# Expert weights fetched in whole rows, eight feature sums open at once, gathers and scatters moved

## The chip, the cores and the metric

One core of one Trainium2 chip runs the whole program in a single launch. The metric is the device time of one execution in microseconds (us). A difference of 0.3% is 12 us here.

## The reference, cut to what matters

The model has two layers over 512 latent tokens and, in the first layer only, 256 context tokens, all of width 1024, in float32. The change touches the last step of each layer, the expert-choice feed-forward:

```python
cap = EC_CAPACITY * N // N_EXPERTS                      # 64 tokens of 512, 32 of 256
aff = softmax(h @ w_router)
gate, idx = lax.top_k(swapaxes(aff, 1, 2), cap)         # each of 16 experts picks its tokens
xe = h[bidx, idx]
hid = silu(xe @ w_gate[e]) * (xe @ w_up[e])             # 1024 -> 1024 features
ye = (hid @ w_down[e]) * gate
return zeros_like(h).at[bidx, idx].add(ye)
```

Each expert's three matrices are 1024 x 1024. In layer 0 an expert handles 64 latent and 32 context tokens (M = 96, `with_ctx`), in layer 1 the 64 latent ones (M = 64).

## The kernel before, in words

The program is a list of phases with a barrier between them; `experts0` and `experts1` are the two that the change touches, both made by `expert_loop(l, with_ctx)`. Each works through 8 pairs of experts: pair 0 is written out, pairs 1 to 6 are a hardware loop on every engine (`Fori`), pair 7 is written out, so that the first pair has no scatters to do and the last no gathers.

**Weights.** SyncE streams them through a ring of 6 slots of 1 MB. A chunk is 256 of a matrix's 1024 columns over all 8 blocks of 128 rows, so each partition gets 8 runs of 1 KB. A pair takes 24 chunks: per expert `e` four times gate and up in turn, then four of down. A slot is loaded again (L1881, L1882) when the matmuls of the chunk in it are done.

**Gate and up (L1960).** Weights are the stationary operand, the gathered tokens `XE` the moving one. One chunk gives two blocks of 128 features; each block is a sum over the 8 row blocks, finished before the next is begun, in a bank of its own that alternates (banks 2, 3 for gate, 4, 5 for up). ScalarE takes silu of gate (L2001) and VectorE multiplies by up into `HT` (L2039) chunk by chunk. In the trace each float32 matmul is two weight loads and two matmul records.

**Down (L1976).** `HT` is stationary, 256 columns of the weights move; ScalarE and VectorE copy each chunk's result out of banks 6 and 7 (L2007 latent rows into `YEL`, L2049 context rows into `YEC`).

**Gather (L1924, L1928; VectorE L2020, L2023).** The tokens of the next pair are picked by a matmul of `X` with a selection matrix, one block of 128 features at a time, 4 matmuls and in layer 0 another 2 of the context; VectorE scales and shifts the result into `XE`. Two gathers, into banks 0 and 1, follow each down chunk of the pair's second expert.

**Scatter (L1944; VectorE L2031).** One matmul per 128 tokens and 512 columns puts the previous pair's result back in token order, 12 steps in layer 0 and 8 in layer 1, and VectorE adds it to `YACC`. They follow the gate and up chunks of the pair's first expert, one or two (layer 0) or one (layer 1) at a time, and alternate banks 6 and 7. GpSimd copies their stationary operand `PTCUR` (L2069, L2071).

**Order.** Every hand-over is a counting semaphore in `ex`; `at(x, i, n)` is its value at step n of pair i, and `credit` is how many steps a producer may run ahead, which is the number of buffers: 2 for gathers (`xe`), scatters (`added`) and the rest. L2154 is the barrier between phases.

Of the kernel before, what the change touches and what calls it, by code (L numbers as in the profile page):

```python
# [24 lines left out]
P = 128  # L25
D = 1024
# [86 lines left out]
def program(nc, t, upto=None, dumps=()):  # L113

    es = ExitStack()
    with es:
# [1710 lines left out]
        PAIR_CHUNKS = 2 * 3 * D // CW  # L1827
# [3 lines left out]
        def expert_loop(l, with_ctx):  # L1831
# [6 lines left out]
            SIL = [A(18944 + 2 * M * i, 2, M) for i in range(2)]  # L1838
            HT = [A(19328 + KB * M * i, KB, M) for i in range(2)]
# [34 lines left out]
            def load(sp, i, j, free=None):  # L1874
# [3 lines left out]
                src = flat[bass.ds(l * NE + 2 * i + e, 1), :, :, c * CW:(c + 1) * CW].rearrange("a p k n -> (a p) k n")  # L1878
# [3 lines left out]
                sp.dma_start(slot(s), src).then_inc(w_full[s], 16)  # L1882
# [27 lines left out]
            def wslot(j):  # L1910
                return slot(first + j)

            def scatter_steps(q):
                return range(q * NS // 8, (q + 1) * NS // 8)

            def pe():
                def gather(i, k):

                    nc.tensor.wait_ge(ex["xe"], at("xe", i, k + 1))
                    bk = bank[k % 2]
                    for n in range(LT):
                        mm = nc.tensor.matmul(bk[:, 0:2 * CAP_L], X[:, CT + n, k * P:(k + 1) * P],  # L1924
                                              PL[:, n, bass.ds(i * (2 * CAP_L), 2 * CAP_L)], start=n == 0, stop=n == LT - 1)
                    if with_ctx:
                        for n in range(CT):
                            mm = nc.tensor.matmul(bk[:, 2 * CAP_L:2 * M], X[:, n, k * P:(k + 1) * P],  # L1928
                                                  PC[:, n, bass.ds(i * (2 * CAP_C), 2 * CAP_C)], start=n == 0, stop=n == CT - 1)
                    mm.then_inc(ex["gather"], 1)  # L1930

                def scatter(i, n):
                    tl, hf = outs[n]
                    if n == 0:
                        nc.tensor.wait_ge(ex["dl"], at("dl", i, 8 + 2))
                        if with_ctx:
                            nc.tensor.wait_ge(ex["dc"], at("dc", i, 8 + 2))
                        nc.tensor.wait_ge(ex["ptcur"], at("ptcur", i, per["ptcur"]))
                    nc.tensor.wait_ge(ex["added"], at("added", i, n + 1))
                    if tl < CT:  # L1940
                        w, y = PTCUR[0:2 * CAP_C, S_LAT + tl * P:S_LAT + (tl + 1) * P], YEC[0:2 * CAP_C, :]
                    else:
                        w, y = PTCUR[:, (tl - CT) * P:(tl - CT + 1) * P], YEL
                    nc.tensor.matmul(bank[6 + n % 2][:, :], w, y[:, hf * 512:(hf + 1) * 512], start=True,  # L1944
                                     stop=True).then_inc(ex["scatter"], 1)

                def pair(i, first_pair, last_pair):
                    nc.tensor.wait_ge(ex["xe"], at("xe", i, KB + 2))
                    for e in range(2):
                        xe = XE[:, :, e * M:(e + 1) * M]  # L1950
                        for c in range(4):
                            n = 4 * e + c
                            for w, x, free in (("gate", 2, "silu"), ("up", 4, "hid")):
# [9 lines left out]
                                if e == 0 and not first_pair:  # L1963
                                    for m in scatter_steps(2 * c + (w == "up")):
                                        scatter(i - 1, m)
# [285 lines left out]
```

## Time and profile before

| | us |
|---|---|
| median of 3 runs | 4068.06 |
| lowest, highest | 4056.97, 4069.73 |
| span of the profiled execution, first to last instruction | 4066.2 |
| experts of layer 0, first to last gate matmul of pairs 1 to 6 | 1455.33 to 2148.45 |
| layer 1, start of pair 1 in the trace | 3298.71 |

TensorE is busy 86% of the span, VectorE 28%, ScalarE 14%, GpSimd 11%, and 126 GB/s are read on average. In the rows below PE is TensorE's matmul side and PEld its weight loads, DVE is VectorE, ACT ScalarE, POOL GpSimd, SP SyncE. A row of the page or of a group view ends in: busy us, mean ns of one | idle time of the engine before them and what ended it; "issue" is idle time that no recorded wait explains. PEclk is the granted TensorE clock, where 1.00 is 2.4 GHz and 0.50 is 1.2 GHz. No time of a profiled execution other than its span is at hand.

### The profile page before, as it was taken

To read this page: it belongs to the slowest core of one execution; us is meant where nothing else is said; L and a number is where in the kernel's file an instruction comes from. 1 tells how busy PE (TensorE), PEld (TensorE's weight loads), DVE (VectorE), ACT (ScalarE), POOL (GpSimd) and SP (SyncE) were. 2 spreads that over 40 slices of the span, in tenths; PEclk is the share of its full clock that TensorE was granted. 3 is DMA by queue.
4 is the path that set the end of the run, shared out by engine and by line. 5 is a ranking of instruction groups with operands and counts; after the bars stand their busy time and mean duration, and the time that the engine had idled before them with its cause. 6 is when DMAs were issued, how large, how long until landed. Compare 5 with 4: busy or idle time off the path is not lost. (4 is left out here: it accounts for less than half of the span.)

```text
span 4066.2 us, 49080 instructions
## 1 busy us (share of the span) xinstructions
PE 3505.4 (86%) x20674; PEld 2738.5 (67%) x20674; DVE 1128.0 (28%) x2115; ACT 568.3 (14%) x1182; POOL 449.8 (11%) x366
## 2 busy tenths in 40 slices
PE   7989977888798999999999498994665899999995
PEld 2445564877675787888888266573564688888884
DVE  0034413455334111111111507205753211111113
ACT  0123133222201000000000104103110000000000
POOL 0000002454221000000000300002622000000002
PEclk9979988999797899999999799996777799999998
DMA  9200112000033565666767120110000377767773
GB/s 301 92 21 16 42 42 73 1 1 1 26 110 108 176 222 194 219 224 221 235 222 234 57 71 28 35 53 20 1 21 31 127 248 247 247 227 247 245 248 117
DMA packets 495175, 513.43 MB, mean 126 GB/s; under 512 B 13200, under 2 KB 490640, under 8 KB 494608
## 3 DMA queue, kind: packets, MB, share of 16 engines
q1 hardware_dynamic: 487792, 492.93, 37.6%
q10 hardware_dynamic: 6048, 13.57, 0.9%
q0 software_dynamic: 1152, 4.19, 0.3%
q8 instruction: 151, 2.47, 0.3%
q14 instruction: 32, 0.26, 0.0%
HBM read 506.99 MB, written 3.67 MB: 126 GB/s over the span
## 5 line engine op out<-in xcount | busy, mean ns | idle before, releaser
L1960 PEld LDWEIGHTS bank<-arena,ring 128*128 128x128 f32 x8192 | 950.4, 195 | 87.9 <-issue 84.1
L1960 PE MATMUL bank<-arena,ring 128*128 128x96 f32 (+1 forms) x8192 | 954.2, 278 | 26.8 <-issue 19.2
L1976 PE MATMUL bank<-ring,arena 128*96 128x256 f32 (+1 forms) x2048 | 457.3, 381 | 9.6 <-DVE arena L2039 8.5
L1976 PEld LDWEIGHTS bank<-ring,arena 128*96 128x96 f32 (+1 forms) x2048 | 301.8, 150 | 149.2 <-DVE arena L2039 12.2
L2039 DVE TENSOR_TENSOR arena<-arena,bank 128x192 f32<-128x192 f32 (+1 forms) x128 | 41.1, 321 | 1075.3 <-PE bank L1960 1075.3
L1105 PE MATMUL bank<-arena 128*128 128x128 f32 x2208 | 272.7, 284 | 21.4 <-DVE arena L1277 19.7
L1105 PEld LDWEIGHTS bank<-arena 128*128 128x128 f32 x2208 | 265.1, 199 | 27.9 <-issue 24.6
L450 PE MATMUL bank<-arena,ring 128*128 128x384 f32 (+1 forms) x704 | 245.1, 511 | 9.1 <-DVEq L2154 7.7
L450 PEld LDWEIGHTS bank<-arena,ring 128*128 128x128 f32 x704 | 134.8, 192 | 118.6 <-issue 33.9
L330 PE MATMUL bank<-ring,small 128*2 128x256 f32 x768 | 178.0, 387 | 28.5 <-ACT small L276 28.0
L1944 PE MATMUL bank<-arena 128*128 128x512 f32 (+1 forms) x320 | 174.2, 633 | 6.4 <-DVE arena L2031 4.9
L480 PE MATMUL bank<-ring,arena 128*128 128x256 f32 (+1 forms) x800 | 170.4, 375 | 6.9 <-ACTq L2154 6.9
L480 PEld LDWEIGHTS bank<-ring,arena 128*128 128x128 f32 x800 | 151.3, 201 | 26.7 <-ACTq L2154 7.5
L2001 ACT ACTIVATE arena<-bank 128x192 f32<-128x192 f32 (+1 forms) x128 | 39.0, 304 | 897.0 <-PE bank L1960 896.9
L1434 PE MATMUL bank<-arena 128*128 128x128 f32 x608 | 109.6, 342 | 53.8 <-POOL arena L1521 30.9
L1924 PE MATMUL bank<-arena,X 128*128 (+1 forms) x1024 | 138.5, 285 | 14.0 <-DVEq L2013 14.0
L1924 PEld LDWEIGHTS bank<-arena,X 128*128 128x128 f32 x1024 | 127.9, 197 | 30.1 <-POOLq L2154 17.1
L441 DVE COPY arena<-bank 128x384 f32<-128x384 f32 (+4 forms) x60 | 30.3, 505 | 424.0 <-PE bank L450 231.7
L330 PEld LDWEIGHTS bank<-ring,small 128*2 128x2 f32 x768 | 62.6, 86 | 123.6 <-ACT small L276 28.0
L1434 PEld LDWEIGHTS bank<-arena 128*128 128x128 f32 x608 | 97.0, 245 | 65.8 <-POOL arena L1521 41.1
L2007 ACT ACTIVATE arena<-bank 64x256 f32<-64x256 f32 x128 | 48.2, 377 | 658.8 <-PE bank L1976 658.8
L1645 PE MATMUL bank<-ring,arena 128*128 128x256 f32 x640 | 138.7, 379 | 1.4 <-ACTq L2154 1.4
(283 smaller groups left out, 3557.2 us busy)
## 6 DMA issues: line engine op xcount, KB each, us to landing
ring<-in_moe_w_gate_dram SPq DMA_DIRECT2D x128, 1024.0 KB, 5.3
ring<-in_moe_w_up_dram SPq DMA_DIRECT2D x128, 1024.0 KB, 5.2
ring<-in_moe_w_down_dram SPq DMA_DIRECT2D x128, 1024.0 KB, 5.2
ring<-in_w_mod_dram SPq DMA_DIRECT2D x48, 1024.0 KB, 5.3
ring<-in_odd_w_in_dram SPq DMA_DIRECT2D x16, 1024.0 KB, 5.4
ring<-in_even_w_in_dram SPq DMA_DIRECT2D x10, 1024.0 KB, 5.3
ring<-in_even_w_out_dram SPq DMA_DIRECT2D x4, 1024.0 KB, 5.3
arena<-in_rpb_tables_dram POOLq DMA_DIRECT2D x8, 512.0 KB, 4.1
```

Source lines behind the costliest of these rows:

```text
L330: mm = nc.tensor.matmul(bank[banks[i % 2]][0:2, 0:CW], CC[:, k, :], slot(idx)[:, k, :], start=k == 0, stop=k == KB - 1)
L450: mm = nc.tensor.matmul(bk[:, 0:b_ - a], lhs(k), rhs(k, a, b_), start=k == 0, stop=k == kb - 1)
L480: mm = nc.tensor.matmul(bk[:, 0:n], UT[:, k, tl * P:(tl + 1) * P], slot(idx, KB, n)[:, k, :], start=k == 0, stop=k == KB - 1)
L1105: mm = nc.tensor.matmul(heads(out[:, :])[:, h, :], lhs(h), rhs(h), start=start, stop=stop)
L1434: mm = nc.tensor.matmul(heads(out[:, :])[:, h, :], lhs(h), rhs(h), start=start, stop=stop)
L1645: mm = nc.tensor.matmul(bank[i % 8][:, 0:CW], mix(k, tl), slot(idxs[j])[:, k, :], start=k == 0, stop=k == KB - 1)
L1924: mm = nc.tensor.matmul(bk[:, 0:2 * CAP_L], X[:, CT + n, k * P:(k + 1) * P], PL[:, n, bass.ds(i * (2 * CAP_L), 2 * CAP_L)], start=n == 0, ...
L1944: nc.tensor.matmul(bank[6 + n % 2][:, :], w, y[:, hf * 512:(hf + 1) * 512], start=True, stop=True).then_inc(ex["scatter"], 1)
L1960: mm = nc.tensor.matmul(bk[:, f * M:(f + 1) * M], wslot(j)[:, k, f * P:(f + 1) * P], xe[:, k, :], start=k == 0, stop=k == KB - 1)
L1976: mm = nc.tensor.matmul(bank[6 + n % 2][0:M, 0:CW], HT[e][:, f, :], wslot(j)[:, f, :], start=f == 0, stop=f == KB - 1)
L2007: nc.scalar.activation(YEL[e * CAP_L:(e + 1) * CAP_L, c * CW:(c + 1) * CW], bank[6 + n % 2][0:CAP_L, 0:CW], ACT.Copy).then_inc(ex["dl"], 1)
L2039: nc.vector.tensor_tensor(HT[e][:, 2 * c:2 * c + 2, :], SIL[n % 2], bank[4 + n % 2][:, 0:2 * M].rearrange("p (f m) -> p f m", f=2), ALU.mu ...
```

## The change

A chunk is now two of the 8 row blocks over all 1024 columns: two whole rows of 4 KB for each partition, still 1 MB, still 24 chunks in a pair and 6 slots. Each gate or up chunk therefore adds 16 matmuls to all eight feature blocks of its matrix, whose sums stay open together in two banks of four blocks (banks 0, 1 gate; 2, 3 up). Silu and the product run once per expert, as two instructions of four blocks each, after the last chunk. Down uses 512 moving columns per matmul and sums in banks 4 and 5, copied out once per expert.

Bank 6 alone is left to the gathers and bank 7 alone to the scatters, and every credit is 1. Of the scatters all but two (10 of 12, 6 of 8) are spread over the gate and up chunks 1 to 7 of the first expert: in layer 0 one, one, two, one, two, one, two, in layer 1 none and then one each. The last two stand between that expert's last up chunk and its down. Of the 8 gathers four stand between the second expert's last up chunk and its down, and one ahead of each of its down chunks. On VectorE the two products stand ahead of the last two adds, and ahead of all gathered blocks.

The diff, with the removed bodies left out (they are in the functions printed above), and without the lines that only change indentation or a count of steps:

```diff
-            SIL = [A(18944 + 2 * M * i, 2, M) for i in range(2)]
-            HT = [A(19328 + KB * M * i, KB, M) for i in range(2)]
+            SIL, HT = A(18944, KB, M), A(19712, KB, M)
...
-            per = dict(gather=KB, xe=KB, gate=8, up=8, silu=8, hid=8, down=8, dl=8, dc=8 if with_ctx else 0,
+            per = dict(gather=KB, xe=KB, gate=8, up=8, silu=2, hid=2, down=8, dl=2, dc=2 if with_ctx else 0,
                        scatter=NS, added=NS, ptcur=2 if with_ctx else 1)
-            credit = dict(xe=2, silu=2, hid=2, dl=2, dc=2 if with_ctx else 0, added=2)
+            credit = dict(xe=1, silu=1, hid=1, dl=1, dc=1 if with_ctx else 0, added=1)
...
-                src = flat[bass.ds(l * NE + 2 * i + e, 1), :, :, c * CW:(c + 1) * CW].rearrange("a p k n -> (a p) k n")
+                src = flat[bass.ds(l * NE + 2 * i + e, 1), :, 2 * c:2 * c + 2, :].rearrange("a p k n -> (a p) k n")
...
-                sp.dma_start(slot(s), src).then_inc(w_full[s], 16)
+                sp.dma_start(slot(s, 2, D), src).then_inc(w_full[s], 16)
...
+            GAP_STEPS = 2
+            EARLY = NS - GAP_STEPS
+            def early_steps(q):
+                return range((q - 1) * EARLY // 7, q * EARLY // 7) if q else range(0)
+            def gather(i, k):
+                nc.tensor.wait_ge(ex["xe"], at("xe", i, k + 1))
+                bk = bank[6]
...
+                nc.tensor.matmul(bank[7][:, :], w, y[:, hf * 512:(hf + 1) * 512], start=True,
+                                 stop=True).then_inc(ex["scatter"], 1)
...
+                def gate_up(i, e, first_pair):
+                    xe = XE[:, :, e * M:(e + 1) * M]
+                    for j in range(4):
+                        for w, x, free in (("gate", 0, "silu"), ("up", 2, "hid")):
+                            c = 12 * e + 2 * j + (w == "up")
+                            wait_w(i, c)
+                            if j == 0:
+                                nc.tensor.wait_ge(ex[free], at(free, i, e + 1))
+                            for kk in range(2):
+                                k = 2 * j + kk
+                                for f in range(KB):
+                                    mm = nc.tensor.matmul(bank[x + f // 4][:, (f % 4) * M:(f % 4 + 1) * M],
+                                                          wslot(c)[:, kk, f * P:(f + 1) * P], xe[:, k, :],
+                                                          start=k == 0 and f % 4 == 0, stop=k == KB - 1 and f % 4 == 3)
+                            mm.then_inc(ex[w], 1)
+                            if e == 0 and not first_pair:
+                                for m in early_steps(2 * j + (w == "up")):
+                                    scatter(i - 1, m)
+                def pair(i, first_pair, last_pair):
+                    nc.tensor.wait_ge(ex["xe"], at("xe", i, KB + 1))
+                    for e in range(2):
+                        gate_up(i, e, first_pair)
+                        if e == 0 and not first_pair:
+                            for m in range(EARLY, NS):
+                                scatter(i - 1, m)
+                        if e == 1 and not last_pair:
+                            for k in range(4):
+                                gather(i + 1, k)
+                        nc.tensor.wait_ge(ex["hid"], at("hid", i, e + 1 + 1))
+                        nc.tensor.wait_ge(ex["dl"], at("dl", i, e + 1))
                         if with_ctx:
+                            nc.tensor.wait_ge(ex["dc"], at("dc", i, e + 1))
+                        for j in range(4):
+                            c = 12 * e + 8 + j
+                            if e == 1 and not last_pair:
+                                gather(i + 1, 4 + j)
+                            wait_w(i, c)
+                            for kk in range(2):
+                                f = 2 * j + kk
+                                for hf in range(2):
+                                    mm = nc.tensor.matmul(bank[4 + hf][0:M, :], HT[:, f, :],
+                                                          wslot(c)[:, kk, hf * 512:(hf + 1) * 512],
+                                                          start=f == 0, stop=f == KB - 1)
                             mm.then_inc(ex["down"], 1)
...
+                        nc.scalar.wait_ge(ex["gate"], at("gate", i, 4 * e + 4))
+                        nc.scalar.wait_ge(ex["hid"], at("hid", i, e + 1))
+                        for g in range(2):
+                            ins = nc.scalar.activation(SIL[:, 4 * g:4 * g + 4, :], bank[g][:, 0:4 * M], ACT.Silu)
+                        ins.then_inc(ex["silu"], 1)
+                        nc.scalar.wait_ge(ex["down"], at("down", i, 4 * e + 4))
+                        if e == 0:
+                            nc.scalar.wait_ge(ex["added"], at("added", i, 1))
+                        for hf in range(2):
+                            ins = nc.scalar.activation(YEL[e * CAP_L:(e + 1) * CAP_L, hf * 512:(hf + 1) * 512],
+                                                       bank[4 + hf][0:CAP_L, :], ACT.Copy)
+                        ins.then_inc(ex["dl"], 1)
...
+                nc.vector.tensor_tensor(y, y, bank[7][:, :], ALU.add).then_inc(ex["added"], 1)
...
+                        if e == 0 and not first_pair:
+                            for m in range(EARLY):
+                                add(i - 1, m)
+                        nc.vector.wait_ge(ex["up"], at("up", i, 4 * e + 4))
+                        nc.vector.wait_ge(ex["silu"], at("silu", i, e + 1 + 1))
+                        for g in range(2):
+                            ins = nc.vector.tensor_tensor(HT[:, 4 * g:4 * g + 4, :], SIL[:, 4 * g:4 * g + 4, :],
+                                                          bank[2 + g][:, 0:4 * M].rearrange("p (f m) -> p f m", f=4), ALU.mult)
+                        ins.then_inc(ex["hid"], 1)
+                        if e == 0 and not first_pair:
+                            for m in range(EARLY, NS):
+                                add(i - 1, m)
+                        if e == 1 and not last_pair:
+                            for k in range(KB):
+                                gathered(i + 1, k)
+                        if with_ctx:
+                            nc.vector.wait_ge(ex["down"], at("down", i, 4 * e + 4))
+                            if e == 0:
+                                nc.vector.wait_ge(ex["added"], at("added", i, 1))
+                            for hf in range(2):
+                                ins = nc.vector.tensor_copy(YEC[e * CAP_C:(e + 1) * CAP_C, hf * 512:(hf + 1) * 512],
+                                                            bank[4 + hf][CAP_L:M, :])
+                            ins.then_inc(ex["dc"], 1)
...
```

## Rows read from the trace of the kernel before

**Rows 1.** The page, costliest groups: gate and up.

```profile
L1960 PE MATMUL bank<-arena,ring 128*128 128x96 f32 (+1 forms) x8192 | 954.2, 278 | 26.8 <-issue 19.2
```

**Rows 2.** Windows of layer 0: scatter stage, down, second expert's gate/up, down with gathers.

```profile
core 0: us, PE busy (x) PEld busy (x) DVE busy (x) ACT busy (x) POOL busy (x), PEclk, DMA share, GB/s
2148.45:2190.05 41.60, 41.13 (x280) 32.85 (x281) 8.43 (x15) 1.33 (x4) 0.00 (x0) 1.00 0.59 192
1497.30:1511.11 13.81, 13.81 (x65) 10.46 (x64) 1.94 (x4) 1.13 (x3) 0.95 (x2) 1.00 0.77 254
1511.11:1540.37 29.26, 28.72 (x257) 28.55 (x256) 1.84 (x5) 1.70 (x5) 0.00 (x0) 1.00 0.92 297
2123.05:2148.45 25.40, 24.64 (x161) 21.23 (x161) 6.97 (x20) 2.79 (x5) 0.00 (x0) 1.00 0.63 199
```

**Rows 3.** Windows of layer 1: scatter stage, down with gathers.

```profile
3298.71:3334.58 35.87, 35.72 (x272) 31.54 (x273) 5.47 (x12) 2.40 (x5) 0.00 (x0) 1.00 0.71 226
3377.80:3400.88 23.08, 22.39 (x129) 15.89 (x129) 3.28 (x8) 1.50 (x4) 0.00 (x0) 1.00 0.65 208
```

**Rows 4.** SyncE's waits, 3400 to 3500 us: for whom, total, times, longest.

```profile
SPq L1881 <- PE bank L1960: 56.4, 16, 5.6
```

**Rows 5.** Windows of whole pairs: six of layer 0, its second; two of layer 1.

```profile
1455.33:2148.45 693.12, 665.03 (x4561) 572.69 (x4561) 114.58 (x264) 41.69 (x102) 5.70 (x12) 0.97 0.68 219
1568.77:1688.92 120.15, 114.79 (x760) 98.51 (x761) 19.10 (x44) 6.95 (x17) 0.95 (x2) 0.94 0.65 211
3400.88:3503.04 102.16, 100.85 (x721) 84.77 (x721) 10.48 (x24) 6.52 (x17) 0.61 (x1) 1.00 0.76 246
3605.20:3713.94 108.74, 107.43 (x720) 90.24 (x721) 10.53 (x24) 6.52 (x17) 0.61 (x1) 0.94 0.71 231
```

**Rows 6.** Timeline where the loop turns, layer 0: start, us, instruction, idle before.

```profile
1799.65 0.56 PE L1928 MATMUL bank<-arena,X 128*128 x4
1804.38 0.95 PE L1960 MATMUL bank<-arena,ring 128*128 128x96 f32 x3 [4.17 <-issue]
```

**Rows 7.** The same, layer 1.

```profile
3400.88 1.32 PE L1960 MATMUL bank<-arena,ring 128*128 128x64 f32 x10 [0.69 <-DVE arena L2020]
```

**Rows 8.** DMA queues, one turn of the loop: layer 0 (two rows), layer 1.

```profile
q1 hardware_dynamic: 24960, 25.17, 67.7%
q8 instruction: 9, 0.15, 0.5%
...
q1 hardware_dynamic: 24949, 25.16, 76.5%
```

**Rows 9.** Timeline of a scatter that waits for an add, layer 0.

```profile
2178.21 1.30 DVE L2031 TENSOR_TENSOR arena<-arena,bank 128x512 f32<-128x512 f32 x2
2178.94 0.30 PEld L1944 LDWEIGHTS bank<-arena 128*128 128x128 f32 x2 [0.99 <-DVE arena L2031]
2180.11 0.69 DVE L2031 TENSOR_TENSOR arena<-arena,bank 128x512 f32<-128x512 f32 x1 [0.59 <-PE bank L1944]
```

**Rows 10.** Timeline of gathers: layer 1 from matmul to VectorE; layer 0's two VectorE steps.

```profile
3398.14 1.86 PEld L1924 LDWEIGHTS bank<-arena,X 128*128 128x128 f32 x16 [0.39 <-issue]
...
3399.34 0.41 DVE L2020 TENSOR_SCALAR arena<-bank,small 128x128 f32<-128x128 f32 x1 [4.28 <-PE bank L1924]
...
1798.91 0.41 DVE L2020 TENSOR_SCALAR arena<-bank,small 128x128 f32<-128x128 f32 x1 [0.87 <-PE bank L1928]
1799.23 0.34 DVE L2023 TENSOR_SCALAR arena<-bank,small 128x64 f32<-128x64 f32 x1
```

**Rows 11.** Groups of 1804.38 to 1920.04: the product with up.

```profile
L2039 DVE TENSOR_TENSOR arena<-arena,bank 128x192 f32<-128x192 f32 x8 | 2.8, 355 | 64.2 <-PE bank L1960 64.2
```

**Rows 12.** Windows: first gathers of layers 0 and 1, final scatters of layer 0.

```profile
1343.68:1357.41 13.73, 12.98 (x96) 12.84 (x96) 5.29 (x16) 1.28 (x1) 0.95 (x2) 0.84 0.00 1
3193.05:3203.32 10.27, 9.77 (x64) 9.58 (x64) 3.28 (x8) 0.00 (x0) 0.61 (x1) 0.76 0.01 2
2247.60:2259.90 12.30, 11.49 (x24) 3.65 (x24) 8.24 (x12) 0.00 (x0) 0.00 (x0) 1.00 0.33 103
```

More of the change, by code:

```diff
@@ L1826, in program @@
                                           "scatter", "added", "ptcur")}
[L1827 removed]
+        PAIR_CHUNKS = 2 * 3 * KB // 2
         ex_base = {x: 0 for x in ex}
@@ L1910, in wslot @@
             def wslot(j):
[L1911 to L1925, printed above, removed]
-                    if with_ctx:
[L1927 to L1935, printed above, removed]
-                        if with_ctx:
[L1937 to L1953, printed above, removed]
-                                j = 12 * e + 2 * c + (w == "up")
-                                wait_w(i, j)
-                                nc.tensor.wait_ge(ex[free], at(free, i, n + 1))
-                                bk = bank[x + n % 2]
-                                for f in range(2):
-                                    for k in range(KB):
-                                        mm = nc.tensor.matmul(bk[:, f * M:(f + 1) * M], wslot(j)[:, k, f * P:(f + 1) * P],
-                                                              xe[:, k, :], start=k == 0, stop=k == KB - 1)
-                                mm.then_inc(ex[w], 1)
-                                if e == 0 and not first_pair:
-                                    for m in scatter_steps(2 * c + (w == "up")):
-                                        scatter(i - 1, m)
-                        nc.tensor.wait_ge(ex["hid"], at("hid", i, 4 * e + 4 + 2))
-                        for c in range(4):
-                            n, j = 4 * e + c, 12 * e + 8 + c
-                            wait_w(i, j)
-                            nc.tensor.wait_ge(ex["dl"], at("dl", i, n + 1))
-                            if with_ctx:
-                                nc.tensor.wait_ge(ex["dc"], at("dc", i, n + 1))
-                            if n < 2:
-                                nc.tensor.wait_ge(ex["added"], at("added", i, 1 + n))
-                            for f in range(KB):
-                                mm = nc.tensor.matmul(bank[6 + n % 2][0:M, 0:CW], HT[e][:, f, :], wslot(j)[:, f, :],
-                                                      start=f == 0, stop=f == KB - 1)
@@ new lines, in wslot @@
+                return slot(first + j, 2, D)
+            GAP_STEPS = 2
[5 more added lines that the diff above has]
+                bk = bank[6]
+                for n in range(LT):
+                    mm = nc.tensor.matmul(bk[:, 0:2 * CAP_L], X[:, CT + n, k * P:(k + 1) * P],
+                                          PL[:, n, bass.ds(i * (2 * CAP_L), 2 * CAP_L)], start=n == 0, stop=n == LT - 1)
+                if with_ctx:
+                    for n in range(CT):
+                        mm = nc.tensor.matmul(bk[:, 2 * CAP_L:2 * M], X[:, n, k * P:(k + 1) * P],
+                                              PC[:, n, bass.ds(i * (2 * CAP_C), 2 * CAP_C)], start=n == 0, stop=n == CT - 1)
+                mm.then_inc(ex["gather"], 1)
@@ L1978, in pair @@
                             mm.then_inc(ex["down"], 1)
-                            if e == 1 and not last_pair:
-                                gather(i + 1, 2 * c)
-                                gather(i + 1, 2 * c + 1)
                 for k in range(KB):
@@ L1990, in pe, with act_features @@
                     scatter(NP - 1, n)
-            def act():
+            def act_features():
                 for x in ("silu", "dl"):
```

81 lines of the change are left out of this document (31 added, 50 removed).

## The prediction

> **What bounds the kernel now.** I read the costliest groups first, then the windows stage by stage, then the timeline where TensorE pauses. Gate and up are the largest group, 8192 matmul records [rows 1], and in the stages that the change touches TensorE is busy nearly throughout: 28.72 us of 29.26 in the second expert's gate and up, 13.81 of 13.81 in down [rows 2]. So a pair costs its count of records times the pace of one. 28.72 over 257 records is 0.112 us for gate and up, and it is the same with 96 moving columns (layer 0) and 64 (layer 1), so the 128-column weight load behind each record sets it, not the columns. Down goes at 13.81 / 64 = 0.216 us for 256 columns. The transfers are not the bound: SyncE's waits in layer 1 are for matmuls that free a slot [rows 4], and the DMA engines are at most 92% busy in any stage shown [rows 2]. Two costs come on top in layer 0. At the loop's turn TensorE idles 4.17 us with no wait that explains it [rows 6], against 0.69 us in layer 1 [rows 7]; and behind it the granted clock is 0.5 for a while, which gives whole pairs of 120.15 us at a mean clock of 0.94 [rows 5]. A clean pair is the sum of its four stages, 41.60 + 13.81 + 29.26 + 25.40 = 110.1 us [rows 2]. Six took 693.12 us [rows 5], so the five turns and the slow clock behind them cost 693.1 - 660.4 = 32.7 us. At 3.1 to 3.5 us a turn, some 16 are idling and 17 are clock.
>
> **Records.** Gate and up keep 256 matmuls a pair (512 records), stationary 128 columns, moving 64 or 96: 28.7 us per expert as before. Down has half the records with twice the columns: 32 x 0.43 = 13.8 us, as before. A scatter is two records of 512 columns, 0.86 us; a gather 12 records in layer 0 (1.34 us) and 8 in layer 1 (0.90). Their numbers don't change. What changes is who waits.
>
> **Transfers in whole rows.** Zero: no wait of TensorE ends on a transfer, so quicker ones only lengthen SyncE's waits. If some wait were hidden there all the same, the idle time of the stage with the busiest queues bounds the gain, 0.5 us of 29.26 [rows 2].
>
> **Silu and product once per expert.** Silu waits for the last gate chunk and has the last up chunk, 28.7 / 8 = 3.6 us, as cover; ScalarE's whole work in that stage is 1.70 us [rows 2]. The product is exposed: it was one of 192 columns, 0.355 us [rows 11]. The add of 512 columns takes 0.69 [rows 9], so 1.05 ns a column and 0.56 us for each of the two of 384: +0.7 us where nothing else covers it (+0.5 in layer 1).
>
> **Scatters on one bank.** Now scatter, add, scatter is a chain. From weight load to add 2180.11 - 2178.94 = 1.17 us, the add 0.69, back 0.04 [rows 9]: 1.90 us for 0.86 of work, 1.04 idle. Layer 0 has it after the doubles at chunks 3 and 5 and three times in the run of four at the end of the stage (the products fit between adds and cost nothing there): 28.7 + 12 x 0.86 + 5 x 1.04 = 44.2 us against 41.60, **+2.6**. Layer 1: 28.7 + 8 x 0.86 + 2 x 1.04 = 37.7 against 35.87 [rows 3], **+1.8**.
>
> **Gathers on one bank.** In layer 1 a gather takes 3399.34 - 3398.14 = 1.20 us to VectorE (0.90 of records, 0.30 of hand-over), VectorE 0.41, back 0.04: 1.65. Layer 0: 1.64 + (1799.57 - 1798.91) + 0.04 = 2.34 us, 1.00 of it idle [rows 10]. The first four stand back to back and the fifth waits for the fourth; the others have a down chunk as cover. VectorE's products come first but end within the first gather. Second expert, layer 0: 28.7 + 4 x 2.34 + 4 x 1.34 + 13.8 + 0.2 for the turn, where no gather is waited for any more, = 57.5 against 29.26 + 25.40, **+2.8**. Layer 1: 28.7 + 4 x 1.65 + 4 x 0.90 + 13.8 + 0.2 = 52.9 against 29.3 + 23.08 [rows 3], **+0.5**.
>
> **The ends of each loop.** First pair: 0.7 + 2.8 = 3.5 and 0.5 + 0.5 = 1.0. Last: 2.6 + 0.7 = 3.3 and 1.8 + 0.5 = 2.3. Final scatters: 12 x 1.90 = 22.8 against 12.30 [rows 12], +10.5; layer 1 8 x (1.90 - 1.02) = +7.0. First gathers: at full clock 8 x 2.34 = 18.7 against 13.73 (+5.0) and 8 x 1.65 = 13.2 against 10.27 (+2.9). But they begin at half clock (means 0.84 and 0.76 [rows 12]), and it rose under back-to-back matmuls. With 40% idling I take it that it stays low: each gather 1.34 or 0.90 longer, +15.7 and +10.1.
>
> **The stall at the turn.** In a turn of layer 0 the instruction queue fetches 9 blocks of 16 KB, in layer 1 none [rows 8]: the loop of layer 1, 720 + 720 records, stays resident, that of layer 0, 760 + 760 [rows 5], does not. After, layer 0 has 256 + 32 + 48 + 12 = 348 matmuls, 1392 records and no more waits than before, less than the 1440 that stayed. So the fetches and the stall go: -32.7 with their clock. Bounds: 0 and -32.7; I take the latter.
> The Trainium skill (Runtime: NRT & Kernel Launch, Instruction fetch mechanics) gives TensorE room for 2048 instructions, but also says that a taken branch outside two fetched blocks forces a fetch. By the first the stall goes; by the second it stays and the sum is 32.7 us higher. Layer 1's loop, six blocks long without a fetch, speaks for the first.
>
> **New slow clock.** Four gathers at 57% busy in a row, once a pair of layer 0, are a pause of 9 us like none in its stages now. The old stalls cost 17 us of clock in six pairs, 2.9 a pair; I take the same price for seven: +20. Bounds: 0 and twice that. Layer 1's gathers are shorter; there I take none.
>
> **Sum.** Layer 0: 6 x 5.4 + 3.5 + 3.3 + 10.5 + 15.7 = 65.4. Layer 1: 6 x 2.3 + 1.0 + 2.3 + 7.0 + 10.1 = 34.2. Less 32.7, plus 20: +86.9. The profiled span is 4066.2, so 4153.1; the median lies 1.9 above the span: **4155 us**, slower.
>
> **Rivals.**
> A, the clock holds: gathers and scatters in chains are enough to keep or bring full clock. For it: a pair of layer 1 ran at 1.00 with its turn's pause [rows 5]. Then first gathers +7.9 in place of +25.8 and no +20: +49, 4117 us.
> B, the layer 0 loop still isn't resident: 32.7 more, 4188 us. For it: I don't know where the limit between 1440 and 1520 records lies, nor what alignment does.
> C, layer 1's first pair at half clock: it has no scatters, and nothing but 64-column matmuls for 28.7 us. If its low start isn't ended there, that stage doubles: +28.7, 4184 us. For it: the pair at 0.94 lost 6.6 us [rows 5].
> D, faster by the pace of records: if 0.112 us comes from successive sums into the same columns, eight open sums end it. The columns alone would take 0.216 / 256 = 0.84 ns each, 0.081 and 0.054 us: 4096 x 0.031 + 4096 x 0.058 = 365 us less, 3790. It decides from 87 / 8192 = 0.011 us a record. Against it: 64 and 96 columns have one pace, which the accumulation would not give.
> E, faster because single banks cost nothing: then all chains vanish and only the stall counts, 4035 us. The Trainium skill (TensorE: Matmul & The Clock Gate, HAM oscillation) reports a thin kernel in which a second PSUM buffer gained nothing; by it this would be the case. Here a scatter visibly waits 0.99 us for the add before it [rows 9].
>
> **Chances.** Forecast 0.58, A 0.15, B 0.09, C 0.10, D 0.05, E 0.03. D and E are faster (0.08); 0.03 of A, with chains much shorter than I reckon, ends within 0.3%, about what a measurement can tell (12 us); slower 0.89. Range: A less a third of its chain costs (82 / 3) is 4090, rounded down to 4085; forecast with B or C and some clock more, 4225.
>
> **What would show it.** Right: a wait of about 1 us ahead of each of the second to fifth gather; scatter starts 1.9 us apart; no instruction fetches in layer 0's loop and under 1 us at its turn; gate and up at 0.112 us; pairs of 115 to 120 us in layer 0 and 104.5 in layer 1. Wrong: another pace of records, a wait for a weight slot, clock at 1.00 through the gathers, or fetches that stay.

## The result and the profile after

The changed kernel takes **4196.85 us** (median of 4 runs, 4195.92 to 4197.97) against 4068.89 on the same chip (4056.97 to 4073.71, 4 runs): ratio 1.0318, 95% interval 1.0302 to 1.0334, 128 us slower. The profiled execution took 4196.67, its span 4194.6. The forecast was 4155 with a range of 4085 to 4225: sign and range right, 42 us short.

The traces before and after, and those of the experiments, are divided at the same places. In brackets stands how much of a stage passed at half clock, in us:

| us | before | changed | gathers on two banks | scatters on two banks | both | before + 100 waits + order |
|---|---|---|---|---|---|---|
| start | 1343.7 | 1340.4 | 1342.9 | 1336.8 | 1342.3 | 1345.9 |
| L0 first gathers | 13.7 [4.4] | 28.6 [28.6] | 13.6 [4.1] | 28.6 [28.6] | 13.6 [4.1] | 13.6 [4.1] |
| L0 first pair | 97.9 | 105.2 [9.6] | 96.7 | 105.1 [9.4] | 96.7 | 96.2 |
| L0 six pairs | 693.1 [37.5] | 710.0 [34.1] | 676.1 [10.2] | 675.9 [27.3] | 641.2 [0] | 652.1 [0] |
| L0 last pair | 99.2 | 105.8 [3.4] | 107.4 [6.8] | 99.2 | 99.2 | 99.1 |
| L0 final scatters | 12.2 | 32.3 [28.8] | 33.2 [32.0] | 12.2 | 12.2 | 12.2 |
| between the layers | 933.2 | 935.5 | 935.7 | 935.0 | 935.9 | 931.5 |
| L1 first gathers | 10.3 [5.0] | 20.6 [20.6] | 10.3 [5.0] | 20.6 [20.6] | 9.9 [4.1] | 10.3 [5.0] |
| L1 first pair | 95.4 | 125.4 [59.5] | 94.3 | 125.3 [59.3] | 94.3 | 94.0 |
| L1 six pairs | 619.4 [13.7] | 633.1 | 614.7 | 621.7 | 603.2 | 604.4 |
| L1 last pair | 93.5 | 96.4 | 96.4 | 94.5 | 94.5 | 93.5 |
| L1 final scatters | 8.4 | 15.2 | 15.2 | 8.4 | 8.4 | 8.4 |
| rest | 46.2 | 46.2 | 46.2 | 46.2 | 46.0 | 46.0 |

"Start" and "between the layers" hold nothing that was changed, yet "start" alone runs from 1332.9 (the kernel with a padded loop, below) to 1345.9 us; so up to 13 us of any single total explain nothing.

The page's costliest groups of the changed kernel (busy us, mean ns of one | idle before them and what ended it) answer to [rows 1]:

```profile
L1959 PE MATMUL bank<-arena,ring 128*128 128x96 f32 (+1 forms) x8192 | 965.9, 281 | 1.3 <-DVE arena L2030 0.8
L1943 PE MATMUL bank<-arena 128*128 128x512 f32 (+1 forms) x320 | 185.3, 662 | 54.8 <-DVE arena L2038 52.3
L1923 PE MATMUL bank<-arena,X 128*128 (+1 forms) x1024 | 165.6, 311 | 58.3 <-DVE arena L2030 26.6
```

Gate and up have lost nearly all of their 26.8 us of idle time, of which 19.2 were "issue", the stall at the turn. Their busy time has grown by 11.7, which I put down to the clock. Scatters now idle 54.8 us, 52.3 of it for VectorE's add, and gathers 58.3 us, 44.3 of it for VectorE to take the block before and 14.0 ahead of the first gather of each layer. No large wait ends on a transfer.

Windows of the changed kernel, in order: scatter stage of layer 0, its down, the second expert's gate and up; the eight gathers with the second down, in the pair before and in this one; then layer 1's scatter stage, its second expert, and the whole of that pair. They answer to [rows 2, 3, 5]:

```profile
core 0: us, PE busy (x) PEld busy (x) DVE busy (x) ACT busy (x) POOL busy (x), PEclk, DMA share, GB/s
1591.55:1636.76 45.21, 41.31 (x281) 32.67 (x280) 9.78 (x15) 3.23 (x5) 0.00 (x0) 1.00 0.63 209
1636.76:1650.49 13.73, 13.73 (x33) 5.24 (x32) 0.69 (x1) 0.00 (x0) 0.95 (x2) 1.00 0.60 192
1650.49:1679.05 28.56, 28.56 (x257) 28.55 (x256) 1.29 (x2) 1.95 (x4) 0.00 (x0) 1.00 0.88 296
1563.31:1591.55 28.24, 25.22 (x130) 16.26 (x129) 6.32 (x18) 0.00 (x0) 0.00 (x0) 1.00 0.48 166
1679.05:1711.76 32.71, 29.69 (x131) 19.34 (x129) 6.31 (x18) 0.00 (x0) 0.00 (x0) 0.84 0.40 141
3509.28:3547.02 37.74, 36.18 (x274) 31.38 (x273) 5.47 (x9) 3.01 (x5) 0.00 (x0) 1.00 0.74 250
3560.89:3614.80 53.91, 51.89 (x354) 40.39 (x353) 4.03 (x10) 1.73 (x4) 0.00 (x0) 1.00 0.73 242
3509.28:3614.80 105.52, 101.94 (x658) 76.06 (x657) 10.20 (x20) 4.74 (x9) 0.61 (x1) 1.00 0.72 238
```

Gate and up keep 28.56 / 256 = 0.112 us a record, with eight sums open as with one. The two windows of gathers and down are the same work in two pairs, 28.24 at full clock and 32.71 at a mean of 0.84.

The timeline of the changed kernel (start, us, instruction, idle before and what ended it), first scatters, then gathers:

```profile
1515.50 0.69 DVE L2038 TENSOR_TENSOR arena<-arena,bank 128x512 f32<-128x512 f32 x1 [3.74 <-PE bank L1943]
1516.24 0.30 PEld L1943 LDWEIGHTS bank<-arena 128*128 128x128 f32 x2 [1.61 <-DVE arena L2038]
1517.40 0.69 DVE L2038 TENSOR_TENSOR arena<-arena,bank 128x512 f32<-128x512 f32 x1 [1.22 <-PE bank L1943]
...
1565.54 1.16 PE L1923 MATMUL bank<-arena,X 128*128 x8 [0.76 <-DVE arena L2030]
1567.85 1.16 PE L1923 MATMUL bank<-arena,X 128*128 x8 [0.76 <-DVE arena L2030]
```

Each add starts 1.90 us after the last, each gather 2.31 us after the last: the chains are as forecast (1.90, 2.34).

Windows of the changed kernel where the clock is low: first gathers of layer 0, the start of the first pair behind them, layer 0's final scatters, first gathers of layer 1, the first pair's first gate and up there, that whole pair; and layer 1's final scatters, where it is not:

```profile
core 0: us, PE busy (x) PEld busy (x) DVE busy (x) ACT busy (x) POOL busy (x), PEclk, DMA share, GB/s
1340.35:1368.96 28.61, 22.56 (x96) 21.06 (x97) 5.29 (x16) 0.00 (x0) 0.94 (x2) 0.50 0.00 1
1368.96:1375.18 6.22, 6.22 (x29) 6.22 (x30) 0.00 (x0) 0.00 (x0) 0.00 (x0) 0.50 0.00 0
2289.94:2322.20 32.26, 22.95 (x24) 5.55 (x24) 8.26 (x12) 0.00 (x0) 0.00 (x0) 0.55 0.10 32
3257.72:3278.33 20.61, 16.57 (x65) 14.22 (x65) 3.28 (x8) 0.00 (x0) 0.61 (x1) 0.50 0.00 0
3278.33:3334.05 55.72, 54.88 (x257) 54.69 (x257) 0.75 (x2) 1.94 (x3) 0.00 (x0) 0.50 0.41 132
3278.33:3403.75 125.42, 122.47 (x640) 99.84 (x640) 4.79 (x12) 3.67 (x7) 0.00 (x0) 0.76 0.58 193
4133.25:4148.44 15.19, 9.00 (x16) 2.38 (x16) 5.49 (x8) 0.00 (x0) 0.00 (x0) 1.00 0.00 0
```

Both layers' first pairs begin at half clock. In layer 0 it rose 6.22 us into the first gate and up, whose matmuls move 96 columns. In layer 1, where they move 64, all 55.72 us of the first gate and up ran at 0.50 with TensorE 98% busy.

DMA queues over the six pairs of layer 0 (packets, MB, share of 16 engines), first the kernel before, then the changed one:

```profile
q8 instruction: 52, 0.85, 0.5%
```

```profile
q8 instruction: 6, 0.10, 0.1%
```

All but 6 of the instruction fetches are gone, and at the turn only 0.27 us before the weight load is idle "issue":

```profile
1591.13 0.19 PEld L1959 LDWEIGHTS bank<-arena,ring 128*128 128x128 f32 x1 [0.27 <-issue]
1591.55 1.70 PE L1959 MATMUL bank<-arena,ring 128*128 128x96 f32 x14
```

### The profile page after: what moved, and what is told of

Its sections match the earlier page's. It is cut to its first block and busy times, and to the rows that moved or that the text cites. A ratio compares the mean times of both kernels' runs of the same rounds, so it can differ in the third digit from the quotient of the medians.

```text
span 4194.6 us, 46254 instructions
## 1 busy us (share of the span) xinstructions
PE 3571.9 (85%) x19650; PEld 2624.6 (63%) x19650; DVE 1116.9 (27%) x2019; ACT 540.0 (13%) x1054; POOL 449.7 (11%) x366
## 3 DMA queue, kind: packets, MB, share of 16 engines
q1 hardware_dynamic: 192880, 492.93, 35.2%
## 5 line engine op out<-in xcount | busy, mean ns | idle before, releaser
L1959 PEld LDWEIGHTS bank<-arena,ring 128*128 128x128 f32 x8192 | 962.6, 198 | 64.2 <-issue 62.4
L1959 PE MATMUL bank<-arena,ring 128*128 128x96 f32 (+1 forms) x8192 | 965.9, 281 | 1.3 <-DVE arena L2030 0.8
L1989 PE MATMUL bank<-ring,arena 128*96 128x512 f32 (+1 forms) x1024 | 462.1, 603 | 3.9 <-DVE arena L2053 3.9
L1989 PEld LDWEIGHTS bank<-ring,arena 128*96 128x96 f32 (+1 forms) x1024 | 151.0, 153 | 266.5 <-issue 258.6
L1105 PEld LDWEIGHTS bank<-arena 128*128 128x128 f32 x2208 | 264.3, 198 | 27.9 <-issue 24.6
L2038 DVE TENSOR_TENSOR arena<-arena,bank 128x512 f32<-128x512 f32 x160 | 110.0, 688 | 549.8 <-PE bank L1943 549.8
L450 PE MATMUL bank<-arena,ring 128*128 128x384 f32 (+1 forms) x704 | 244.0, 509 | 10.3 <-DVEq L2169 8.7
L1943 PE MATMUL bank<-arena 128*128 128x512 f32 (+1 forms) x320 | 185.3, 662 | 54.8 <-DVE arena L2038 52.3
L1923 PE MATMUL bank<-arena,X 128*128 (+1 forms) x1024 | 165.6, 311 | 58.3 <-DVE arena L2030 26.6
L450 PEld LDWEIGHTS bank<-arena,ring 128*128 128x128 f32 x704 | 134.3, 191 | 118.9 <-issue 33.0
L1923 PEld LDWEIGHTS bank<-arena,X 128*128 128x128 f32 x1024 | 143.8, 215 | 101.6 <-DVE arena L2030 30.8
L330 PE MATMUL bank<-ring,small 128*2 128x256 f32 x768 | 178.3, 387 | 28.6 <-ACT small L276 28.0
L2053 DVE TENSOR_TENSOR arena<-arena,bank 128x384 f32<-128x384 f32 (+1 forms) x64 | 28.2, 483 | 643.5 <-PE bank L1959 643.5
L1434 PE MATMUL bank<-arena 128*128 128x128 f32 x608 | 109.5, 342 | 53.9 <-POOL arena L1521 30.9
L2027 DVE TENSOR_SCALAR arena<-bank,small 128x128 f32<-128x128 f32 x128 | 52.5, 410 | 324.4 <-PE bank L1927 176.2
```

What stands on the lines that cost most here:

```text
L330: mm = nc.tensor.matmul(bank[banks[i % 2]][0:2, 0:CW], CC[:, k, :], slot(idx)[:, k, :], start=k == 0, stop=k == KB - 1)
L450: mm = nc.tensor.matmul(bk[:, 0:b_ - a], lhs(k), rhs(k, a, b_), start=k == 0, stop=k == kb - 1)
L1105: mm = nc.tensor.matmul(heads(out[:, :])[:, h, :], lhs(h), rhs(h), start=start, stop=stop)
L1434: mm = nc.tensor.matmul(heads(out[:, :])[:, h, :], lhs(h), rhs(h), start=start, stop=stop)
L1943: nc.tensor.matmul(bank[7][:, :], w, y[:, hf * 512:(hf + 1) * 512], start=True, stop=True).then_inc(ex["scatter"], 1)
L1959: mm = nc.tensor.matmul(bank[x + f // 4][:, (f % 4) * M:(f % 4 + 1) * M], wslot(c)[:, kk, f * P:(f + 1) * P], xe[:, k, :], start=k == 0 an ...
```

## The experiments

All start from the changed kernel unless said otherwise; ratios are to the kernel before on the same chip.

**First gathers on two banks.** Is layer 1's slow first pair caused by the first gathers, as rival C had it, or by its own order?

```diff
-                bk = bank[6]
+                bk = bank[4 if isinstance(i, int) and i == 0 and k % 2 else 6]
```

VectorE reads the same bank, and the wait of these gathers is one step looser to match.

> Only the first eight gathers of each layer are changed: they alternate two banks (one of down's, free at that time) instead of one, with one more allowed ahead. Theory (idling in the chain keeps the clock low, and the low clock is carried into the first pair): layer 0's first gathers fall from 28.6 us to about 14, layer 1's from 20.6 to about 10, the clock rises during them as in the kernel before, and with it layer 1's first pair falls from 125.4 to about 98 us and layer 0's by about 4: 56 us less in all, 4141 us. Rival (the first pair of layer 1 is slow by its own doing, with eight open sums and no scatters): only the first gathers gain, 25 us less, 4172 us.

4138.92 us, ratio 1.018 (1.0163 to 1.0197). Windows of this kernel, first gathers of layers 0 and 1, and layer 1's first pair:

```profile
core 0: us, PE busy (x) PEld busy (x) DVE busy (x) ACT busy (x) POOL busy (x), PEclk, DMA share, GB/s
1342.28:1356.01 13.73, 12.98 (x96) 12.84 (x96) 5.29 (x16) 0.00 (x0) 0.95 (x2) 0.84 0.00 1
3239.32:3249.65 10.33, 9.83 (x65) 9.64 (x65) 3.28 (x8) 0.00 (x0) 0.61 (x1) 0.75 0.00 0
3249.65:3347.13 97.48, 94.53 (x640) 73.34 (x640) 4.79 (x12) 3.67 (x7) 0.00 (x0) 1.00 0.73 248
```

Sixteen gathers made denser return 25.2 us in themselves and 27.9 in layer 1's first pair, whose own instructions are unchanged. So that pair's slow clock comes from the chain before it.

**Gathers on two banks throughout.** Which share of the loss is theirs?

```diff
-            credit = dict(xe=1, silu=1, hid=1, dl=1, dc=1 if with_ctx else 0, added=1)
+            credit = dict(xe=2, silu=1, hid=1, dl=1, dc=1 if with_ctx else 0, added=1)
...
-                bk = bank[6]
+                bk = bank[6 + k % 2]
...
```

VectorE reads the same banks, the second gather waits for the last add in bank 7, and a pair still waits for all eight gathers.

> The changed kernel with two banks (6, 7) and credit 2 for the gathers alone; scatters stay on bank 7 with credit 1. Theory (chain and clock): first gathers 14 and 10 us instead of 28.6 and 20.6, layer 1's first pair under 98 us, the gathers ahead of down 6.7 and 4.6 us instead of 10.5 to 13 and 7.7, and no fall of the clock there; scatter stages 45.2 and 37.7 us and final scatters 32 and 15 us as they are. 110 us less, 4087 us. Rival (the clock falls in the scatter chains, not in the gathers): 40 us less at most beyond the first gathers' 25.

4084.92, ratio 1.0048 (1.003 to 1.0066), 112 us under the changed kernel. The windows of this kernel: six pairs of layer 0, its final scatters.

```profile
core 0: us, PE busy (x) PEld busy (x) DVE busy (x) ACT busy (x) POOL busy (x), PEclk, DMA share, GB/s
1453.21:2129.32 676.11, 652.72 (x4177) 499.52 (x4176) 108.47 (x216) 31.02 (x54) 5.72 (x12) 0.99 0.66 223
2236.75:2269.95 33.20, 23.89 (x24) 5.76 (x24) 8.26 (x12) 0.00 (x0) 0.00 (x0) 0.52 0.10 31
```

The total is close to the expected 4087, and the rival, which allowed 65 us at most, is out. One detail was wrong: the clock still falls in layer 0, 10.2 us in the six pairs, though the gathers are dense.

**Scatters on two banks throughout.**

```diff
-                nc.tensor.matmul(bank[7][:, :], w, y[:, hf * 512:(hf + 1) * 512], start=True,
+                nc.tensor.matmul(bank[6 + n % 2][:, :], w, y[:, hf * 512:(hf + 1) * 512], start=True,
```

Their credit is 2, VectorE's add follows, and the first gather waits for the last add in bank 6.

> The changed kernel with two banks (6, 7) and credit 2 for the scatters alone; gathers stay on bank 6 with credit 1. Theory: scatter stages 40.2 and 35.8 us instead of 45.2 (46.8 with slow clock) and 37.7, final scatters 12 and 8.4 instead of 32.3 and 15.2; gathers, and with them layer 1's slow first pair, as in the changed kernel. 78 us less, 4119 us. With the other half this adds up to the 198 us of both. Rival (two halves of one wait, so that either alone gives little, or either alone gives nearly all): well off that sum.

4109.71, ratio 1.0104 (1.0073 to 1.0135), 87 under the changed kernel. This kernel's six pairs of layer 0, then layer 1's first pair, slow as in the changed one:

```profile
core 0: us, PE busy (x) PEld busy (x) DVE busy (x) ACT busy (x) POOL busy (x), PEclk, DMA share, GB/s
1470.55:2146.41 675.86, 657.69 (x4178) 507.04 (x4176) 107.37 (x216) 31.01 (x54) 5.70 (x12) 0.98 0.66 224
3213.38:3338.69 125.31, 122.35 (x641) 99.79 (x641) 4.79 (x12) 3.67 (x7) 0.00 (x0) 0.76 0.57 193
```

Of the 9 us below expectation (4119) 3.5 are "start"; the rival, well off the sum of the halves, is out.

**Both on two banks**, twice: the edits of both halves together. Nothing else of the change is undone.

> Gathers and scatters both alternate banks 6 and 7 with credit 2, everywhere; they never overlap in time, so two banks serve both. Everything else is the changed kernel. Theory (the loss is the chains on single banks and the slow clock that they bring): layer 0 pairs 118.3 to about 110 us, layer 1 pairs 105.5 to about 102.5, first gathers 14 and 10, final scatters 12 and 8 us, layer 1's first pair about 97; 155 us less in all, 4040 us, and below the kernel before, because the stall at the turn stays away. Rival 1 (single banks cost little; the order and the product once per expert do): 4150 us or more. Rival 2 (the clock in layer 0 falls for another reason, about once a pair): 4060 to 4070.

3998.88 (3990.4 to 4002.56), ratio 0.9829 (0.9813 to 0.9846). And again:

> The changed kernel with two banks and credit 2 for gathers and scatters, once more, beside the next one on the same chip. Expected as before: 3999 us, layer 0 pairs 106.9 us and layer 1 pairs 100.5 us with no fall of the clock in either.

3999.00, ratio 0.9834 (0.9811 to 0.9858). The second of them, six pairs of layer 0 and of layer 1, and one scatter stage of layer 0:

```profile
core 0: us, PE busy (x) PEld busy (x) DVE busy (x) ACT busy (x) POOL busy (x), PEclk, DMA share, GB/s
1452.55:2093.79 641.24, 641.24 (x4178) 495.62 (x4177) 107.37 (x216) 31.01 (x54) 5.72 (x12) 1.00 0.68 236
3245.24:3848.49 603.25, 603.25 (x3937) 455.09 (x3937) 60.39 (x120) 28.45 (x54) 3.70 (x6) 1.00 0.72 250
1559.42:1599.58 40.16, 40.16 (x281) 32.78 (x280) 9.18 (x15) 3.22 (x5) 0.00 (x0) 1.00 0.65 226
```

TensorE is busy for all of 641.24 us at full clock. This version beats both kernels, and the single banks cost 198 us. Their halves add up: 112 + 87 = 199. I had expected 4040. Of the 41 us between, 19 are layer 0's six pairs (106.9 us each against 110), whose falls of the clock I had not expected to go entirely, and 12 are layer 1's (100.5 against 102.5), where the clock had not fallen.

**Short runs again.** The same order of matmuls, but each chunk is fetched in runs of 1 KB as before, so the weights are in the wrong places.

```diff
-                src = flat[bass.ds(l * NE + 2 * i + e, 1), :, 2 * c:2 * c + 2, :].rearrange("a p k n -> (a p) k n")
+                src = flat[bass.ds(l * NE + 2 * i + e, 1), :, :, c * CW:(c + 1) * CW].rearrange("a p k n -> (a p) k n")
```

> The changed kernel, but each 1 MB chunk is fetched as in the kernel before, 256 columns of 1024 in runs of 1 KB, into the same slot. The weights that the matmuls find are therefore in the wrong order and the output is not the reference's; the number and size of all matmuls are unchanged. Theory (no wait ends on a transfer): the same time, 4197 us within 0.3%. Rival (whole rows give something, so that the loss elsewhere is larger than it seems): slower by 15 us or more, with TensorE waiting for slots.

4196.94, ratio 1.032 (1.0302 to 1.0337): no difference. The page's queue row, of the changed kernel and then of this one:

```profile
q1 hardware_dynamic: 192880, 492.93, 35.2%
```

```profile
q1 hardware_dynamic: 487792, 492.93, 36.1%
```

2.5 times the packets raise the engines' share from 35.2 to 36.1% of the span and cost the kernel nothing.

**The loop made as long as before.** Was it length that made the loop of before fetch at each turn?

```diff
+            PAD = 150
...
+                                    at_mm = ((e * 4 + j) * 2 + (w == "up")) * 16 + kk * 8 + f
+                                    if with_ctx and (at_mm + 1) * PAD // 256 > at_mm * PAD // 256:
+                                        nc.tensor.wait_ge(silu_c, 1)
+                                        nc.tensor.wait_ge(first_loaded, 48)
```

150 times a wait that has long been met, spread over layer 0's gate and up.

> The changed kernel with 150 waits on long-passed semaphores spread over layer 0's gate and up matmuls: TensorE's loop in layer 0 has 1587 instructions instead of 1437 (the kernel before: 1585; its layer 1 loop, which was not fetched again: 1497). Theory (the stall at the turn is the fetch of a loop that doesn't stay resident): 9 blocks fetched in each turn again and about 3.2 us more idling at five turns, 16 us, plus up to 17 us of clock: 4213 to 4230 us. Rival (the stall had another cause, such as the gathers right ahead of the turn): no fetches matter, 4197 us.

4192.51 (4182.55 to 4203.08), ratio 1.0321 (1.0302 to 1.034): all four executions lie below the expected range, and length alone doesn't bring the stall back. The queue over the six pairs, and the one late start:

```profile
q8 instruction: 16, 0.26, 0.1%
...
1702.24 1.02 PE L1960 MATMUL bank<-arena,ring 128*128 128x96 f32 x7 [0.60 <-issue]
```

This trace is of the fastest execution, 4182.55; nothing shows whether the others, up to 4203, fetched at more turns. In it the six pairs took 703.1 us, 17.1 at half clock, against 710.0 and 34.1 in the changed kernel: three of the six pairs had no fall of the clock at all. Why is open.

**The loop of before moved, not shortened.** 100 instructions with two such waits each stand ahead of it, in a phase before the experts.

```diff
+            def pe():
+                for _ in range(100):
+                    nc.tensor.wait_ge(silu_c, 1)
+                    nc.tensor.wait_ge(first_loaded, 48)
-            phase("fetch_mla", act=act)
+            phase("fetch_mla", pe=pe, act=act)
```

> The kernel before, with 100 satisfied waits put into a phase in which TensorE has nothing to do, some 400 us ahead of the experts. They move layer 0's loop of 1585 instructions by 0.39 of a block of 256, so that it crosses six of the places at which a fetch was seen to start instead of seven; its order is unchanged. Theory (place and length decide whether the loop stays resident): no fetches in layer 0's turns, no idle time over 1 us there, 33 us less: 4033 us. Rival (length or order alone decides, or the two loops differ in something else): 9 blocks a turn and 4066 us as before.

4035.31 (4029.89 to 4038.76), ratio 0.9918 (0.9892 to 0.9943), as expected. Six pairs of layer 0 of this kernel and its queue there:

```profile
1455.22:2118.70 663.48, 649.87 (x4560) 558.60 (x4561) 114.64 (x264) 41.60 (x102) 5.70 (x12) 1.00 0.70 228
...
q8 instruction: 6, 0.10, 0.1%
```

Moved by 100 instructions, the same loop of 1585 turns with 6 fetches in place of 52 and never falls to half clock: 29.6 of the stall's 32.7 us, with nothing changed in the work. Why this place is better the run doesn't show.

**The kernel before with the new order of gathers.** Two gathers stand ahead of the second expert's down, two behind each of its first three chunks, so that the next pair waits for none.

```diff
+                        if e == 1 and not last_pair:
+                            gather(i + 1, 0)
+                            gather(i + 1, 1)
                         nc.tensor.wait_ge(ex["hid"], at("hid", i, 4 * e + 4 + 2))
...
-                            if e == 1 and not last_pair:
-                                gather(i + 1, 2 * c)
-                                gather(i + 1, 2 * c + 1)
+                            if e == 1 and not last_pair and c < 3:
+                                gather(i + 1, 2 * c + 2)
+                                gather(i + 1, 2 * c + 3)
```

VectorE's steps move with them.

> The kernel before, with each two gathers of its pair loop put ahead of a down chunk instead of behind it, so that the last thing before the turn is a down chunk (8 x 2 records of 0.216 us, 3.5 us of work). Length and place of the loop's instructions are unchanged (1585). Theory (the order decides: TensorE's sequencer reaches the turn while down is still queued, and the fetch lies beside it): the 3.4 to 4.2 us idle at the turn and the slow clock behind it go even if blocks are fetched, 33 us less, and the 0.7 us wait for the product is covered, 5 us less twice: 4025 us. Rival (the length or place of the loop decides alone): the idle time stays at over 2 us and so does the clock, 4055 us or more.

4055.69 (4045.49 to 4060.49), ratio 0.9964 (0.9951 to 0.9977): the rival was right. Layer 1's six pairs fell from 619.4 to 604.4 (6.6 of it is the one pair of before with a fall of the clock), but layer 0's lost 12 us. Layer 0's six pairs, its queue there, and one turn:

```profile
1449.95:2155.06 705.11, 677.59 (x4562) 581.05 (x4560) 114.65 (x264) 41.68 (x102) 5.72 (x12) 0.95 0.66 215
...
q8 instruction: 51, 0.84, 0.5%
...
1680.79 1.46 PE L1960 MATMUL bank<-arena,ring 128*128 128x96 f32 x11 [2.85 <-issue]
```

The fetches stay, and 68.3 us of it pass at half clock (before: 37.5).

**Both small edits on the kernel before**, the order and the move: eight sums and whole rows are left out.

> The kernel before with its columns of 256, its two open sums per bank and all its buffers, and only two edits: gathers one step ahead of down, and the layer 0 loop moved by 100 idle instructions. Theory (all that the changed kernel could gain is the turn of the loop and the cover of the product's wait; whole rows, eight open sums and 512 columns in down give nothing): 4035 us of the moved loop alone less about 3 us for each of layer 0's pairs and 1.5 for each of layer 1's and its 6.6 us of slow clock: 4000 us, the same as the repaired change within 5 us. Rival (the whole-row layout and the open sums are worth something by themselves): 4015 us or more.

4013.42 (4009.32 to 4013.97), ratio 0.9873 (0.9851 to 0.9895): outside the theory's 4000 within 5, and just under the rival's 4015. Six pairs of layer 0, six of layer 1, one scatter stage of layer 0:

```profile
1455.66:2107.76 652.10, 647.19 (x4561) 557.70 (x4560) 114.61 (x264) 41.68 (x102) 5.72 (x12) 1.00 0.70 232
3254.92:3859.32 604.40, 603.49 (x4321) 508.19 (x4321) 62.94 (x144) 39.10 (x102) 3.70 (x6) 1.00 0.76 250
1564.37:1606.22 41.85, 41.04 (x282) 32.75 (x281) 8.77 (x16) 2.98 (x6) 0.00 (x0) 1.00 0.63 205
```

Layer 1 is within 1.2 us of the best version. So the two small edits give 54 us (from 4067.4) where the best version gives 68. Of layer 0's 10.9 us more, 6 x (41.85 - 40.16) = 10.1 lie in the scatter stage, where VectorE has a product per chunk among the adds. That these products delay the adds is my reading; no run isolates it.

## Why the forecast was right in sign and 42 us short

By the table's rows, measured against forecast:

| term | forecast | measured |
|---|---|---|
| first gathers, L0 and L1 | +15.7, +10.1 | +14.9, +10.3 |
| L0 six pairs (chains 32.4, stall -32.7, clock 17.1) | +16.8 | +16.8 |
| L0 first and last pair (with the seventh fall of the clock) | +9.7 | +13.9 |
| L0 final scatters | +10.5 | +20.0 |
| L1 first pair | +1.0 | +30.0 |
| L1 six pairs, last pair, final scatters | +23.1 | +23.5 |
| start and between | 0 | -1.0 |
| sum | +86.9 | +128.4 |

- **Chains.** Mechanism right, and in layer 0 the size: scatter stages 45.21 and 37.74 (forecast 44.2 and 37.7), second expert 28.56 + 28.24 = 56.8 and 53.9 (57.5, 52.9). The run with both on two banks confirms that they are the whole loss, with their clock.
- **Layer 1's six pairs are right by luck.** A pair took 105.52 us against 102.16 before, so the change cost a pair 3.36 us and not 2.3, 20.2 us in six; the second expert alone took 1.0 more than forecast. That the row shows +13.7 is because one of the six pairs before had run partly at half clock (the 6.6 us that the prediction names under rival C), and none did after. The sum had no term for getting that back.
- **Layer 1's first pair, the largest miss (29.0 of 41.5).** The term that failed is "0.5 + 0.5 = 1.0" for that pair: it charges the gathers at half clock and then takes the pair behind them at full clock. It took 30.0 us more. The first gathers at 0.50 flow straight into 64-column matmuls, and the clock rose only 3.8 us into the down of 512 columns. ("Layer 1's gathers are shorter; there I take none" speaks of the gathers ahead of down, and was right: layer 1's six pairs had no fall.) This was rival C, at +28.7, with a chance of 0.10. Of its two conditions the low start was already in the sum; open was only whether 64-column matmuls would end it, and no row of before showed them beginning at half clock. In layer 0 the same low start ended after 6.2 us of 96-column matmuls. Whether the columns make the difference no run isolates.
- **Layer 0's final scatters, mis-sized by 9.5.** Charged 12 x 1.90 at full clock; they ran at 0.55, 32.26 / 12 = 2.69 each. I priced the clock for chains of gathers, but not for this longer one. With scatters on two banks it took 12.2.
- **L0's first and last pair, 4.2.** They passed 9.6 + 3.4 = 13.0 us at half clock, 6.5 lost, where the forecast allowed one fall, 2.9, for both. 6.2 of the 9.6 were carried over from the first gathers.
- **Clock in the six pairs.** 34.1 us at half clock are 17 lost, where 17.1 was taken. The size is right partly by luck: with gathers on two banks 10.2 remain, with scatters on two banks 27.3, so both chains feed it, and I had named the gathers alone.
- **Stall.** -32.7 is right in effect: 52 fetches became 6. The reason given, 1392 records being fewer than the 1440 that stayed, isn't: a loop of 1585 instructions (1520 records and 65 others) turns without the stall once it is moved. That the place matters is shown; by which rule is not. By the Trainium skill (Runtime: NRT & Kernel Launch, Instruction fetch mechanics) a block is 256 instructions, so the move by 100 is 0.39 of a block. Counted in the traces, TensorE begins the loop of before after 13438 instructions and fetches 52 blocks in six pairs, the moved one after 13538 and fetches 6, and the padded one, 2 instructions longer, after 13441 and fetches 16. The first and the last lie almost alike, so no rule by place and length alone is likely to cover all three. Of the skill's two rules for TensorE the room for 2048 instructions agrees with the moved loop; the fetch for a taken branch outside two blocks does not, since 1585 instructions, over six blocks, turned without one.
- **Zero terms.** Whole rows: zero, shown. Pace of records: 0.112, unchanged, so rival D is out. Silu and product once: inside the stages, not isolated.
- **Rivals.** A fell with the clock at 0.50 in the first gathers, E with the 198 us that single banks cost, B with the 6 fetches. What the change can gain did come once the chains were gone and was worth 68 us (4067.4 to 3999.0 on one chip); single banks took 198.

What stays open: why the padded loop hardly fetches, why the clock falls in some pairs of layer 0 and not in others of the same order, and why the same chain of scatters ran at full clock for all its 15.19 us in layer 1 while layer 0's fell to half after some 3.5 us.

## What to carry to other kernels

A buffer count is a pace: before giving six of the eight banks to open sums, add up the round trip (matmul, hand-over, VectorE, back) of each stream left with one, here 1.90 and 2.31 us for 0.86 and 1.34 of work. Where a sparse chain precedes a dense stage, price the dense stage at half clock too, if the trace shows the clock low as it begins. And where "issue" idles at a hardware loop's turn with instruction fetches in the queue, move the loop before rewriting it: 100 idle waits ahead of it were worth 30 us.

## What the runs showed of the hardware that was not expected

- The same loop of 1585 instructions fetched 52 blocks in six pairs in one place and 6 in another, 100 instructions further: 693.1 against 663.5 us.
- At half clock, 55.72 us of 64-column float32 matmuls with TensorE 98% busy did not raise the clock, where in layer 0 it rose within 6.22 us of 96-column ones; behind denser gathers the same matmuls began at 1.00 and stayed there (97.48 us for the pair, mean clock 1.00). The Trainium skill (TensorE: Matmul & The Clock Gate, What's actually happening) has activity release the throttle; these rows don't agree, as far as busy time is activity.
- Time at half clock isn't in proportion to the pauses: in layer 0's six pairs the kernel before passed 37.5 us at half clock, 68.3 with only the gathers reordered, none with the stall gone; the changed one 34.1, with scatters on two banks 27.3, with gathers on two banks 10.2, with both none.
